# Forget-gate sums subtracted from the scores by an F32R product of 48 rows instead of an fp32 product of 128 rows

## What is computed

```
q, k, v, f_logit = split(h @ w_in)          # 16 heads of 64, one f_logit per head
log_f = log_sigmoid(f_logit + b_f)
c = cumsum(log_f, over positions)           # one row per head
s = q k^T / 8 + c[t] - c[s]                 # masked where s > t
p = softmax(s);  o = p v;  out = o @ w_out
```

## Time and profile before

| | us |
|---|---|
| median of 3 runs | 1978.04 |
| range of the runs | 1976.99 to 1979.93 |
| the profiled execution | 1976.96 |
| its span, first to last instruction | 1975.8 |
| TensorE busy (matmul) | 1809.3, 92% |
| VectorE busy | 651.8, 33% |
| ScalarE busy | 471.1, 24% |
| GpSimd busy | 52.7, 3% |
| mean granted clock of TensorE | 0.97 |

### The profile page before, as it was taken

One profiled execution on the slowest core, in us unless ns is written; L12 is line 12 of the kernel. 1 busy time (PEld: TensorE's weight loads), 2 busy tenths in 40 slices (PEclk: granted clock), 3 DMA queues, 4 the chain that ended last, 5 costly groups with the idle time before them and its releaser, 6 DMA issues.

```text
span 1975.8 us, 22757 instructions
## 1 busy us (share of the span) xinstructions
PE 1809.3 (92%) x8651; PEld 984.3 (50%) x8652; DVE 651.8 (33%) x856; ACT 471.1 (24%) x592; POOL 52.7 (3%) x67
## 2 busy tenths in 40 slices
PE   7989998988899999998689999999999996999996
PEld 6769994475799877554423333332332332333332
DVE  4444442342544412553322222222222222222223
ACT  1435540131444304321011111111111111111111
POOL 0000001000000020230000000000000000000000
PEclk9989998999899999998799999999999998999998
DMA  7334552411455523330599999999999995999995
GB/s 259 138 140 178 187 197 87 148 65 44 155 185 184 200 92 127 128 124 4 220 377 393 429 428 429 428 430 428 429 429 429 428 429 208 375 429 428 429 429 227
DMA packets 84954, 536.97 MB, mean 272 GB/s; under 512 B 8736, under 2 KB 8840, under 8 KB 60328
## 3 DMA queue, kind: packets, MB, share of 16 engines
q1 hardware_dynamic: 79088, 531.64, 66.5%
q10 hardware_dynamic: 5816, 4.59, 0.8%
HBM read 535.17 MB, written 1.05 MB: 271 GB/s over the span
## 4 chain that ended last, share of the span: by engine, by line
PE 68%; DMA 22%; DVE 6%; ACT 2%; issue 2%; ACTq 0%; POOL 0%; SPq 0%; PEldq 0%; DVEq 0%; POOLq 0%
DMA expert_ring<-in_expert_w_up 22%; PE psA L1569 20%; PE psB L678 9%; PE psA L689 9%; PE psB L349 6%; PE psA L362 6%; PE psB L340 6%; PE psA L1074 2%; PE psA L1575 1%; PE psB L741 1%; PE psB L1598 1%; PE psB L324 1%; PE psB L1081 1%; PE psA L1560 1%; PE psA L790 1%
## 5 line engine op out<-in xcount | busy, mean ns | idle before, releaser
L1569 PE MATMUL psA<-expert_ring,gathered_T 128*64 128x512 f32 x1024 | 455.7, 598 | 29.7 <-DMA expert_ring<-in_expert_w_up 29.7
L1570 PE MATMUL psA<-expert_ring,gathered_T 128*64 128x512 f32 x1024 | 455.7, 598 | 0.0
L1569 PEld LDWEIGHTS psA<-expert_ring,gathered_T 128*64 128x64 f32 x1024 | 135.3, 137 | 343.6 <-issue 282.7
L1569 PE MATMUL psA<-expert_ring,activated_T 128*64 128x512 f32 x528 | 241.3, 600 | 2.5 <-ACT activated_T L1784 0.3
L1570 PE MATMUL psA<-expert_ring,activated_T 128*64 128x512 f32 x528 | 241.2, 600 | 0.0
L575 DVE TENSOR_TENSOR w_low<-panel_ring,w_high 128x2048 fp32r<-128x2048 f32 x64 | 146.5, 2292 | 171.8 <-ACT w_high L621 171.8
L621 ACT ACTIVATE w_high<-panel_ring 128x2048 fp32r<-128x2048 f32 x64 | 122.4, 1915 | 179.0 <-PE psB L678 105.0
L1900 DVE TENSOR_SCALAR normed<-psA 128x512 f32<-128x512 f32 x32 | 22.1, 692 | 403.9 <-PE psA L1570 403.9
L678 PE MATMUL psB<-hT_high,w_high 128*128 128x256 f32 x512 | 145.0, 283 | 2.5 <-DVE w_low L575 2.5
L678 PE MATMUL psB<-hT_high,w_low 128*128 128x256 f32 x512 | 144.9, 283 | 0.0
L678 PE MATMUL psB<-hT_low,w_high 128*128 128x256 f32 x512 | 144.9, 283 | 0.0
(11 more groups left out here) (404 smaller groups left out, 2293.5 us busy)
## 6 DMA issues: line engine op xcount, KB each, us to landing
expert_ring<-in_expert_w_up SPq DMA_DIRECT2D x128, 2048.0 KB, 25.4
expert_ring<-in_expert_w_down SPq DMA_DIRECT2D x64, 2048.0 KB, 22.3
panel_ring<-in_mlp_w SPq DMA_DIRECT2D x32, 2048.0 KB, 8.2
panel_ring<-in_w_in SPq DMA_DIRECT2D x11, 2048.0 KB, 7.9
panel_ring<-in_fox_w_in SPq DMA_DIRECT2D x6, 2048.0 KB, 7.8
panel_ring<-in_lru_w_in SPq DMA_DIRECT2D x4, 2048.0 KB, 16.8
panel_ring<-in_lru_w_out SPq DMA_DIRECT2D x2, 2048.0 KB, 7.9
panel_ring<-in_fox_w_out SPq DMA_DIRECT2D x2, 2048.0 KB, 7.9
```

The source lines that it names most:

```text
L1569: M.matmul(ps[0:SLOTS], lhsT, rhs[0], **flags)
L1570: return M.matmul(ps[SLOTS:P], lhsT, rhs[1], **flags)
```

## The change

`cT`, `c_sel` and the work tiles shrink from 128 to 48 rows. w_f and b_f are loaded twice, into columns (rows) 0 to 15 and 32 to 47, with zeros between, so that the gate sums come out in rows 0 to 15 and again in rows 32 to 47. ScalarE copies the 48 rows to F32R (the high part), and VectorE overwrites rows 32 to 47 with the fp32 sums less this high part (the low part). `c_sel` is F32R with -1 in rows h and 32 + h, so that one product subtracts both parts. These transfers have a semaphore of their own (`f_loaded`), and the thresholds of `late` fall by 32.

```diff
+LOW, GATES = 32, 32 + NH
@@ FoxTiles
-        self.c_sel = sb("minus_head_row", [P, NH, P])
-        self.cT = sb("cum_log_f", [P, T])
+        self.c_sel = k.sb("minus_head_row", [GATES, NH, P], F32R, ctx=c)
+        self.cT = sb("cum_log_f", [GATES, T])
+        self.c_parts = k.sb("cum_log_f_parts", [GATES, T], F32R, ctx=c)
...
-        self.wf = sb("w_f", [P, KD, NH])
-        self.bf = sb("b_f", [NH, 1])
+        self.wf = sb("w_f", [P, KD, GATES])
+        self.bf = sb("b_f", [GATES, 1])
...
-        self.lf = sb("log_f_work", [NH, 2, T])
+        self.lf = sb("log_f_work", [GATES, 2, T])
@@ fox_pool
-    G.memset(f.c_sel[:], 0.0).then_inc(*pool.step())
+    G.memset(f.c_sel[:].bitcast(F32), 0.0).then_inc(*pool.step())
     G.memset(f.mask[:], 0.0).then_inc(*pool.step())
-    G.memset(f.cT[:], 0.0).then_inc(*pool.step())
+    G.memset(f.wf[:], 0.0).then_inc(s.f_zeroed, 1)
+    G.memset(f.bf[:], 0.0).then_inc(s.f_zeroed, 1)
     G.wait_ge(*pool.last())
-    G.affine_select(out=f.c_sel[:], in_=f.c_sel[:], compare_op=ALU.not_equal, fill=-1.0, base=0,
+    G.affine_select(out=f.c_sel[:], in_=f.c_sel[:].bitcast(F32), compare_op=ALU.not_equal, fill=-1.0, base=0,
+                    pattern=[[-1, NH], [0, P]], channel_multiplier=1).then_inc(*pool.step())
+    G.wait_ge(*pool.last())
+    G.affine_select(out=f.c_sel[:], in_=f.c_sel[:].bitcast(F32), compare_op=ALU.not_equal, fill=-1.0, base=-LOW,
                     pattern=[[-1, NH], [0, P]], channel_multiplier=1).then_inc(s.fox_masks, 1)
@@ fox_pe
-        last = M.matmul(k.psA[0:NH, 0, 0:T], f.wf[:, c, :], k.hT[:, c, :], start=(c == 0), stop=(c == KD - 1))
+        last = M.matmul(k.psA[0:GATES, 0, 0:T], f.wf[:, c, :], k.hT[:, c, :], start=(c == 0), stop=(c == KD - 1))
...
-                    last = M.matmul(out, f.c_sel[:, h, :], f.cT[:, 0:s1], start=False, stop=True)
+                    last = M.matmul(out, f.c_sel[:, h, :], f.c_parts[:, 0:s1], start=False, stop=True)
@@ fox_act
-        A.dma_start(f.bf[:], a["fox_b_f"][0].rearrange("(n o) -> n o", o=1)).then_inc(s.late, 16)
-    A.dma_start(f.wf[:], a["fox_w_in"][0][:, 3 * D:].rearrange("(k p) n -> p k n", p=P)).then_inc(s.late, 16)
+        A.wait_ge(s.f_zeroed, 2)
+        for at in (0, LOW):
+            A.dma_start(f.bf[at:at + NH], a["fox_b_f"][0].rearrange("(n o) -> n o", o=1)).then_inc(s.f_loaded, 16)
+    for at in (0, LOW):
+        A.dma_start(f.wf[:, :, at:at + NH], a["fox_w_in"][0][:, 3 * D:].rearrange("(k p) n -> p k n", p=P)).then_inc(
+            s.f_loaded, 16)
...
     A.activation(y, ms, ACT.Sqrt).then_inc(s.qk_root, 1)
+    A.wait_ge(s.c_summed, 1)
+    A.activation(f.c_parts[:], f.cT[:], ACT.Copy).then_inc(s.c_high, 1)
@@ fox_dve
-    one = k.ones[0:NH, 0:1].to_broadcast([NH, T])
-    V.tensor_tensor_scan(f.cT[0:NH, :], one, f.lf[:, 1, :], 0.0, ALU.mult, ALU.add).then_inc(s.cum_f, 1)
+    one = k.ones[0:GATES, 0:1].to_broadcast([GATES, T])
+    V.tensor_tensor_scan(f.cT[:], one, f.lf[:, 1, :], 0.0, ALU.mult, ALU.add).then_inc(s.c_summed, 1)
...
     newton_rsqrt(V, dve, ms, y, t)
+    V.wait_ge(s.c_high, 1)
+    V.tensor_tensor(f.c_parts[LOW:], f.cT[LOW:], f.c_parts[LOW:].bitcast(F32), ALU.subtract).then_inc(s.cum_f, 1)
```

More of the change, by code:

```diff
@@ L94, in __init__ @@
             sem("cum_f_ready"), sem("qk_variance"), sem("qk_rooted"), sem("qk_normed"))
+        self.f_zeroed, self.f_loaded, self.c_summed, self.c_high = (
+            sem("f_zeroed"), sem("f_loaded"), sem("c_summed"), sem("c_high"))
         self.nat_T, self.nat_evicted = sem("transposed"), sem("transpose_evicted")
@@ L762, in fox_pe @@
         project_nat(k, FOX + j, k.psB[j % 2])
-    M.wait_ge(s.late, 96)
+    M.wait_ge(s.f_loaded, 64)
     M.wait_ge(s.x_updated, 4)
     for c in range(KD):
-        last = M.matmul(k.psA[0:NH, 0, 0:T], f.wf[:, c, :], k.hT[:, c, :], start=(c == 0), stop=(c == KD - 1))
+        last = M.matmul(k.psA[0:GATES, 0, 0:T], f.wf[:, c, :], k.hT[:, c, :], start=(c == 0), stop=(c == KD - 1))
     last.then_inc(s.f_products, 1)
@@ L827, in fox_act @@
         evict(j)
-    fps = k.psA[0:NH, 0, 0:T]
+    fps = k.psA[0:GATES, 0, 0:T]
     A.wait_ge(s.f_products, 1)
-    A.wait_ge(s.late, 96)
+    A.wait_ge(s.f_loaded, 64)
     A.activation(f.lf[:, 0, :], fps, ACT.Abs, bias=f.bf[:]).then_inc(s.f_read, 1)
@@ L867, in fox_dve @@
     V.wait_ge(s.f_read, 1)
-    V.wait_ge(s.late, 96)
-    V.tensor_scalar(f.lf[:, 1, :], k.psA[0:NH, 0, 0:T], f.bf[:], 0.0, ALU.add, ALU.min).then_inc(*dve.step())
+    V.wait_ge(s.f_loaded, 64)
+    V.tensor_scalar(f.lf[:, 1, :], k.psA[0:GATES, 0, 0:T], f.bf[:], 0.0, ALU.add, ALU.min).then_inc(*dve.step())
     V.wait_ge(*dve.last())
@@ L1341, in hybrid_dve @@
     V.wait_ge(*dve.last())
-    V.wait_ge(s.late, 112)
+    V.wait_ge(s.late, 80)
     V.tensor_tensor(h.o_hg[:], h.o_hg[:], h.gn[:].unsqueeze(1).to_broadcast([P, TT, HGW]), ALU.mult).then_inc(*dve.step())
@@ L1430, in expert_panel @@
     return k.ring[:, EXPERT_SLOTS[odd][j], :].rearrange("p (k n) -> p k n", k=2 if j < 4 else 4)
-LATE_MOE, BIASES = 112 + 64, 16 * (SMALL_LOADS + 5)
+LATE_MOE, BIASES = 80 + 64, 16 * (SMALL_LOADS + 5)
 def moe_pool(k, m):
```

## The result

| | before | after |
|---|---|---|
| median, us | 1977.51 (4 runs) | 2002.8 (4 runs) |
| all runs, us | 1975.36 to 1979.93 | 1996.4, 1997.04, 2008.57, 2009.72 |
| ratio, 95% interval | | 1.0131 [1.0100, 1.0162] |
| profiled execution, its span | 1976.96, 1975.8 | 1997.04, 1995.9 |
| mean granted clock | 0.970 | 0.960 |

The change costs 25.3 us, 1.3%. The forecast was 1985.5 with a range up to 1998: the direction is right, the size is a third of what came, and the median lies above the range. The profiled execution is one of the two shorter ones; the four runs of the kernel after lie 13 us apart, where those of before lie 5 apart. That spread is part of the story.

A forecast was written before the change was run, and what follows sets the result against it. TensorE's products, pair after pair of heads, were taken to bound the attention; preparation 0, shape changes net of savings +4.5 and a later clock rise +3.0 made +7.5 us, a median of 1985.5, range 1972 to 1998.

The forecast's parts named there:

- The preparation: Before the attention: extra transfers, copy and subtraction stay hidden under 15.8 us of cover and cost 0.
- The change of shape: Attention scores: switching between 128 and 48 rows costs 0.41 us a round trip; net of F32R savings, +4.5 us in all.
- The clock: Attention: thinner pairs delay the rise to full clock until the third pair's scores, +3.0 us.
- bound of +25: Attention: upper bound on the clock's cost if the rise never comes in this stage, +25 us.
- a clock that stays low for most of the loop: Rival, attention: half clock for most of the loop, +12 to +30 us, 1990 to 2008; chance 0.13.
- A changed time behind the attention: Sign, after the attention: any changed time there, other than the clock's, would be outside the prediction's account.
- Only the switches: Rival, attention: shape changes cost but the clock rises as before, +4.5 us, 1982.5; chance 0.28.
- No switch: Rival, attention: 48 rows run like 128, or switch without draining, -4.8 us, 1973.2; chance 0.22.
- Two passes for F32R: Rival, attention gate product: F32R of 48 rows takes two passes, +10 to +13 us, near 1990; within the remainder's 0.04.

The follow-up runs named there:

- second execution: The kernel after run once more unaltered, profiled: this execution took 2008.36 us; its four runs have median 2003.65, ratio 1.0124 to the kernel before.
- kernels of 128 rows: The kernel after with 128 instead of 48 gate rows, still F32R: 1974.64 us, ratio 0.9993; variants with unread products added: 1977.64, 1974.41 and 1972.47 us.
- filler at the tail: Kernel after with 128 rows, four unread products in the wait for the keys and four more before the last transposes: 1974.41 us, ratio 0.9979.
- kernels made from after: Ten profiled executions of the kernel after and its variants, against before and its two fillers: experts 975.9 to 981.9 us, where those three take 976.7, 972.0, 973.0.
- filled kernel: The kernel after with four unread fp32 products of 512 columns in TensorE's wait for the transposed keys: 1981.72 us, ratio 1.0022 to the kernel before.

## Why the prediction was off in size

**The preparation: right.** Nothing of it reaches TensorE; the end of the second normalisation moved by 0.6 us under a cover of 15.

**The change of shape: right, and near in size.** Put at 0.41 us a round trip and 5.3 us a pair; measured 0.36 (0.41 where it stands alone) and 5.17. At full clock on both sides the stage grows by 4.4 us, for which +4.5 stood in the sum. That they agree so closely is partly luck: the pairs behind the first bring 0.6 us each, 3.5 in all, where 4.3 was forecast, and the first pair and the tail bring the other 0.9, where 0.2 stood.
**The clock: the step that failed.** "I take a rise in the third pair's scores" gave +3.0. In the profiled execution the stage grew by 15.3, of which 4.4 are the shape and 10.8 the clock, and the rise came two pairs later, in the fifth pair's scores. In the second execution it never came in the loop: 31.1 - 4.4 = 26.7, a little over the bound of +25 that I had worked out; the case of a clock that stays low for most of the loop I had given 0.13. Over the medians the clock added 15 to 19 us. The mechanism was named; the term was mis-sized by a factor of three and a half in one execution, of nine in the other, and of five to six over the medians. My reason for the early rise was that "transposes and the products of pair 3 follow each other densely there". They do in the executions too, in each pair, and it was not enough. No row showed that transposes lift the clock: in the kernel before it rose at 419.1, behind score products of one shape and before the first transposes at 422.84. The rows I had spoke for the rival: the router, at 0.50 with TensorE busy 7.04 of 8 us, was the one row of thin work that stayed low, and the earlier trace rows of 419:455 only showed that a clock once up stays up.

**Missed outright:** two things behind the attention, which I had taken as they were. One is the low stretch at its end, 13.7 us instead of 6.8. It added 2.0 us up to the second MLP, and in the kernels of 128 rows it gives back part of what the stage wins. Why it is longer after an attention of 41 or 61 us than after one of 46 was not settled; with the filler at the tail it was 6.8 us again. The other is the experts, 2.9 us longer in the profiled execution and 4.8 on average over the kernels made from after. "A changed time behind the attention, other than the clock's, would be outside my account": it goes with a lower clock there, but the attention's pairs do not explain it, and its cause stays open.

**The rivals.** "Only the switches" gave 1982.5; the kernel in which only they are left took 1981.72. That the two lie so near is luck, since the filled kernel also lacks the low first pair (2.6 us in the stage of before) and has the longer experts. "No switch" gave 1973.2 from -4.8; with one shape the stage gave -4.7 and the median 1974.64, but the ratio of 0.9993 does not show the gain. Low clock for most of the loop gave 1990 to 2008: that is what happened in mechanism. Of the eight runs of the kernel, 1994 to 2016, four lie above 2008. Two passes for F32R: refuted by one record of 0.12 us.

## What to carry to other kernels

Keep the rows of alternating products in one shape of the array: here the gate product takes the same 0.06 and 0.12 us with 72 rows as with 128, and with 48 rows it costs a round trip of 0.4 us more. Or put the products of the small shape together: one change per pair instead of four took the loss away. Where a stage begins behind an idle stretch, it can inherit a half clock, and what it loses is set by whether its own pattern can climb; price both cases in full, and weigh the bad one by the nearest stretch that began cold, not by one that was already up. Unread products in the idle stretch in front, placed so that nothing waits behind them, test this in one run. They can be kept, but look where the next idle stretch comes: one of 2.22 us cost the clock again here.

## What the hardware showed that was not expected

- A TensorE that is recorded as busy without a break (419 to 480 in the second execution of after) can stay at 1.2 GHz for 81.9 and, with fp32, for 102.4 us, when products of 48 and 128 rows alternate one by one. The Trainium skill, TensorE: Matmul & The Clock Gate, Part 1, has sustained matmul activity release the throttle. The dense kernel before agrees (up again after 6.8 us); the alternating ones, though recorded as busy, do not.
- The same products in the same order stay at full clock once they have it (1.00 over 43 us in after + filler, from 411 to 454). The state in which the stage began decided, not its work alone.
- An F32R product of 128 columns takes 0.06 us between fp32 products of the same shape; of the weight loads around it only 0.05 us show, in the next product of 256 columns (0.48 us instead of 0.43).
- With shorter score products the loop over VectorE and ScalarE shows in every second pair: 3.77 and 4.56 us in turn.
